# Forgetting attention of a decoder step: prompt and sample attention merged into one loop of 32 steps

## The reference, cut to what matters

```python
# prompt: 512 queries, causal
logits = einsum('bqhd,bkhd->bhqk', qb, k) * FOX_SCALE + cb[..., :, None] - cum[:, :, None, :]
logits = where(q_pos >= k_pos, logits, NEG_INF)
o = einsum('bhqk,bkhd->bqhd', softmax(logits), v)
# samples: 8 sequences x 4 queries against 2048 past keys (16 pages) and 4 new ones
k_past, v_past, lf_past = k_pool[page_table], v_pool[page_table], lf_pool[page_table]
suffix = reverse_cumsum(lf_all) - lf_all
logits = einsum('bqhd,bkhd->bhqk', q, k_all) * FOX_SCALE + suffix[:, :, None, :] - suffix[:, :, p_len:, None]
o = einsum('bhqk,bkhd->bqhd', softmax(where(mask, logits, NEG_INF)), v_all)
```

## Time and profile before

| | us |
|---|---|
| median of three runs | 3816.27 |
| the profiled execution | 3816.24 |
| its span, first to last instruction | 3814.6 |
| attention, first TensorE instruction at L1116 to the output projection's first at L668 | 1061.16 to 1684.47 |

### The profile page before, as it was taken

The page is one execution under the profiler, slowest core; times in us unless marked ns, Lnnn a source line. Parts: engine busy times, 40 slices in busy tenths (PEclk is TensorE's granted clock), DMA queues, the critical chain, the costliest instruction groups (busy, mean ns, idle before and its releaser), DMA issues.

```text
span 3814.6 us, 64314 instructions
## 1 busy us (share of the span) xinstructions
PE 3390.1 (89%) x26621; PEld 3033.2 (80%) x26621; DVE 1572.4 (41%) x2273; ACT 1059.2 (28%) x1437; POOL 240.9 (6%) x279
## 2 busy tenths in 40 slices
PE   7998899998999999988999866279999799889997
PEld 6897799988944466667999754179999698779997
DVE  2324544333134411226442379854432432464423
ACT  3301322222022244433222234342222320232222
POOL 0000000004300000000000057200000000000000
PEclk9996899999966699998999988689999899789998
DMA  3113232313110199962223211023232110422331
GB/s 93 56 34 111 72 88 87 92 53 84 38 48 1 56 377 393 392 246 68 86 87 91 55 44 44 12 67 88 87 91 76 56 51 27 124 70 85 88 91 46
DMA packets 465044, 367.67 MB, mean 96 GB/s; under 512 B 16329, under 2 KB 429438, under 8 KB 464924
## 3 DMA queue, kind: packets, MB, share of 16 engines
q1 hardware_dynamic: 449808, 348.72, 28.4%
q10 hardware_dynamic: 11020, 16.22, 1.2%
q0 software_dynamic: 4096, 1.06, 0.3%
HBM read 348.68 MB, written 17.26 MB: 96 GB/s over the span
## 4 chain that ended last, share of the span: by engine, by line
PE 82%; DVE 9%; issue 4%; ACT 3%; DVEq 0%; POOL 0%; DMA 0%; ACTq 0%; SPq 0%; POOLq 0%
PE acc L668 54%; PE acc L649 6%; PE acc L1005 3%; DVE big L1244 3%; PE acc L952 2%; PE acc L940 2%; PE acc L942 2%; PE acc L975 2%; PE acc L1044 2%; PE acc L864 2%; PE acc L852 1%; DVE rstd L1274 1%; PE acc L728 1%; ACT mix L2176 1%; PE acc L962 1%
## 5 line engine op out<-in xcount | busy, mean ns | idle before, releaser
L668 PE MATMUL acc<-h_hi,wsp 128*128 128x272 f32 x5632 | 943.3, 289 | 65.9 <-DVE h_lo L1530 65.9
L1266 DVE TENSOR_TENSOR wsp<-ring,wsp 128x1024 fp32r<-128x1024 f32 (+1 forms) x320 | 416.9, 1306 | 1164.2 <-ACT wsp L1893 1164.2
L668 PEld LDWEIGHTS acc<-h_hi,wsp 128*128 128x128 f32 x5632 | 797.9, 190 | 68.7 <-issue 68.4
L1893 ACT ACTIVATE wsp<-ring 128x1024 fp32r<-128x1024 f32 (+1 forms) x320 | 358.4, 1124 | 1297.6 <-PE acc L668 1294.5
L668 PE MATMUL acc<-h_lo,wsp 128*128 128x272 f32 x3328 | 690.0, 289 | 0.0
L668 PEld LDWEIGHTS acc<-h_lo,wsp 128*128 128x128 f32 x3328 | 527.3, 190 | 0.0
L668 PE MATMUL acc<-g_hi,wsp 128*128 128x272 f32 x2816 | 473.5, 290 | 24.0 <-DVE g_lo L1525 24.0
L668 PEld LDWEIGHTS acc<-g_hi,wsp 128*128 128x128 f32 x2816 | 400.9, 190 | 24.9 <-issue 24.9
L668 PE MATMUL acc<-i_hi,wsp 128*128 128x272 f32 x1536 | 265.1, 295 | 37.2 <-DVE i_lo L1294 32.4
L668 PE MATMUL acc<-g_lo,wsp 128*128 128x272 f32 x1408 | 292.4, 289 | 0.0
L668 PEld LDWEIGHTS acc<-i_hi,wsp 128*128 128x128 f32 x1536 | 224.8, 195 | 39.6 <-issue 35.5
(11 more groups left out here) (287 smaller groups left out, 3442.0 us busy)
## 6 DMA issues: line engine op xcount, KB each, us to landing
ring<-in_ffn_w SPq DMA_DIRECT2D x176, 512.0 KB, 3.8
mix<-in_cache_fox_k SPq DMA_DIRECT2D x96, 512.0 KB, 9.5
mix<-in_cache_fox_v SPq DMA_DIRECT2D x96, 512.0 KB, 10.2
ring<-in_ffn_w SPq DMA_DIRECT2D x64, 704.0 KB, 4.5
big<-in_cache_fox_k SPq DMA_DIRECT2D x32, 512.0 KB, 8.5
big<-in_cache_fox_v SPq DMA_DIRECT2D x32, 512.0 KB, 13.1
ring<-in_conv_w SPq DMA_DIRECT2D x24, 512.0 KB, 3.9
ring<-in_gla_wr SPq DMA_DIRECT2D x16, 512.0 KB, 3.7
```

Source lines behind the costliest of these rows:

```text
L668: last = pe.matmul(acc[:, bank + h, 0:HALF], wsp[:, s, w, k * P:(k + 1) * P], rhs[:, k0 + k, h * HALF:(h + 1) * HALF], start=start and k = ...
L1266: dve.tensor_tensor(wsp[:, s, 1, 0:tiles * P], ring[:, slot, 0:tiles * P], wsp[:, s, 0, 0:tiles * P], ALU.subtract).then_inc(wlo_done, 1)
L1893: act.activation(wsp[:, slot % SPLITS, 0, 0:tiles * P], ring[:, slot, 0:tiles * P], ACT.Copy)\
```

## The change

The two stages become one loop of 32 steps and 4 more. A step takes one pair of prompt items (two heads, one query block; the query blocks are now the outer loop, so the first 8 steps have 128 keys, the next 8 256, then 384 and 512) and four key pages of one sequence, and weighs the four value pages of four steps earlier. Of a key page, VectorE transposes 32 x 32 blocks (`turn_pages`), so that a head's 64 features lie in two blocks, and the scores of four pages come from 128 products of 32 rows and 32 columns of the array, 16 places in all (`sample_scores`). The forget sums come from a table `bias_all`, made once ahead of the loop and added by four products of 32 rows. The queries are repeated over the four partition groups and laid out in zeroed blocks by GpSimd (`query_blocks`), once for each sequence. The pages share a ring of 7 places, of which 5 are the weights' `ring`; the load of the output projection's weights now waits until all value pages are used. The mask of the prompt is added by a product with the identity instead of on VectorE; the scaling by the reciprocal moves to the copy of the result. Loops over sequences are written out.

```diff
 # SyncE
+for s in range(STEPS + LAG):
+    for g in range(GR):
+        if s < STEPS:
+            k_at[s * GR + g] = len(sequence)
+            sequence.append(("k", s * GR + g))
+        if s >= LAG:
+            v_at[(s - LAG) * GR + g] = len(sequence)
+            sequence.append(("v", (s - LAG) * GR + g))
 ...
+        for n, (kind, page) in enumerate(sequence):
+            if page % GR == 0:
+                sp.load(regs[kind], pt_sb[0:1, page:page + GR])
+                numbers[kind] = [sp.snap(r, min_val=0, max_val=NPOOL - 1) for r in regs[kind]]
+            if n >= RAW:
+                last_kind, last_page = sequence[n - RAW]
+                sp.wait_ge(turned if last_kind == "k" else v_used, last_page + 1)
+            cache = cache_k if kind == "k" else cache_v
+            sp.dma_start(raw(n), cache[0, ds(numbers[kind][page % GR], 1)].rearrange("a p h d -> p (a h d)"))\
+              .then_inc(raw_in[n % RAW], 16)
+        sp.wait_ge(v_used, DB * NPAGES)
                 load_out(w_view(fox_wo[0]))
 # TensorE
+    def scores_of_pair(s):
+        n = item(2 * s)[2]
+        q = n // P - 1
+        if s:
+            pe.wait_ge(pv_out, 2 * s)
 ...
+        for x in range(2):
+            h = item(2 * s + x)[1]
+            rows = slice(DH * x, DH * (x + 1))
+            pe.matmul(acc[:, 6 + x, 0:n], big[rows, h // 2, q * P:(q + 1) * P], big[rows, KD + h // 2, 0:n],
+                      start=True, stop=False, skip_group_check=True)
+        for x in range(2):
+            h = item(2 * s + x)[1]
+            pe.matmul(acc[:, 6 + x, 0:n], ident[0:FH, h:h + 1].to_broadcast([FH, P]), ncum[:, 0:n],
+                      start=False, stop=False, skip_group_check=True)
+            pe.matmul(acc[:, 6 + x, q * P:n], ident[:], causal[:], start=False, stop=True,
+                      skip_group_check=True).then_inc(sc_full, 1)
 ...
+    def sample_scores(s):
+        b, G = s // NG, s % NG
+        half = slice(32 * (b // 2), 32 * (b // 2 + 1))
+        pe.wait_ge(ksc_out, s)
+        pe.wait_ge(turned, GR * (s + 1))
+        if G == 0:
+            pe.wait_ge(qz_done, b + 2)
+        for a in range(GR):
+            at = a * NPAGES * 32 + G * P
+            pe.matmul(acc[:, a, 0:P], pick[half, b % 2].rearrange("p h i -> p (h i)"), bias_all[half, at:at + P],
+                      start=True, stop=False, skip_group_check=True, tile_position=(32 * (b // 2), 0))
 ...
+        for c in range(GH4):
+            for f in range(2):
+                cell = 2 * c + f
+                for a in range(GR):
+                    quad = slice(32 * a, 32 * (a + 1))
+                    for j in range(GR):
+                        h = GH4 * j + c
+                        at = (2 * h + f) * 32
+                        last = pe.matmul(acc[32 * j:32 * (j + 1), a, 0:P], qz[quad, b % 2, h, f, :],
+                                         kT[quad, :, at:at + 32], start=False, stop=(cell == 2 * GH4 - 1),
+                                         skip_group_check=True, tile_position=(32 * a, 32 * j))
 ...
+        last.then_inc(ksc_full, 1)
 ...
+    def weigh(v):
+        b, u = v // NG, v % NG
 ...
+        pe.wait_ge(pt_out, v + 1)
+        for g in range(GR):
+            page = v * GR + g
+            pe.wait_ge(*landed(v_at[page]))
+            for j in range(GR):
+                at = g * P + 32 * j
+                last = pe.matmul(acc[32 * j:32 * (j + 1), 5, 0:256], ptb[:, v % 2, at:at + 32],
+                                 raw(v_at[page])[:, j * 256:(j + 1) * 256], start=False,
+                                 stop=(u == NG - 1 and g == GR - 1), skip_group_check=True,
+                                 tile_position=(0, 32 * j))
+            last.then_inc(v_used, 1)
 ...
+    def attention():
+        for s in range(STEPS + LAG):
+            v = s - LAG
+            if s < STEPS:
+                if s % KD == 0 and s:
+                    rows_to_tiles(s)
+                scores_of_pair(s)
+            elif s == STEPS:
+                rows_to_tiles(s)
+            if v >= 0:
+                turn(v)
+            if v > 0 and v % NG == 0:
+                output(v // NG - 1)
+            if v >= 0:
+                weigh(v)
+            if s < STEPS:
+                sample_scores(s)
+                turn_pair(s)
+            if s < STEPS:
+                values_of_pair(s)
+        output(DB - 1)
 # VectorE
+    def turn_pages(s):
+        dve.wait_ge(ksc_full, s)
+        for g in range(GR):
+            n = k_at[s * GR + g]
+            dve.wait_ge(*landed(n))
+            dve.transpose(kT[:, g, :], raw(n)).then_inc(turned, 1)
+    def attention():
+        for s in range(STEPS + LAG):
+            v = s - LAG
+            if s < STEPS:
+                b, G = s // NG, s % NG
+                for x in range(2):
+                    n = item(2 * s + x)[2]
+                    dve.wait_ge(sc_full, 2 * s + x + 1)
+                    dve.tensor_reduce(nmax[:, x:x + 1], acc[:, 6 + x, 0:n], AX.X, ALU.max, negate=True)\
+                       .then_inc(pmax_done, 1)
+                dve.wait_ge(ksc_out, s + 1)
+                z = zs[b % 2]
 ...
+                step(dve.tensor_reduce(mx[:, b % 2, G:G + 1], z[:, G * GR * PAGE:(G + 1) * GR * PAGE], AX.X, ALU.max))
 ...
+                for x in range(2):
+                    dve.wait_ge(pexp_done, 2 * s + x + 1)
+                    dve.reciprocal(rsum[:, x:x + 1], rsum[:, x:x + 1]).then_inc(rinv_done, 1)
+                if s + 1 < STEPS:
+                    turn_pages(s + 1)
 ...
 # ScalarE
+        for s in range(STEPS + LAG):
+            v = s - LAG
+            if s < STEPS:
+                for x in range(2):
+                    n = item(2 * s + x)[2]
+                    act.wait_ge(pmax_done, 2 * s + x + 1)
+                    act.activation(probs[x][:, 0:n], acc[:, 6 + x, 0:n], ACT.Exp, bias=nmax[:, x:x + 1],
+                                   accum_out=rsum[:, x:x + 1]).then_inc(pexp_done, 1)
+            if v >= 0:
 ...
+                act.wait_ge(pt_full, v + 1)
+                if v >= 2:
+                    act.wait_ge(v_used, GR * (v - 1))
+                act.activation(ptb[:, v % 2, :], acc[:, 4, :], ACT.Copy).then_inc(pt_out, 1)
+            if s < STEPS:
+                b, G = s // NG, s % NG
+                z = zs[b % 2]
+                act.wait_ge(ksc_full, s + 1)
 ...
+                act.activation(z[:, G * GR * PAGE:(G + 1) * GR * PAGE].rearrange("p (g a s) -> p a g s", g=GR, a=GR),
+                               acc[:, 0:GR, 0:P].rearrange("p a (g s) -> p a g s", g=GR), ACT.Copy)\
+                   .then_inc(ksc_out, 1)
 ...
+                for x in range(2):
+                    n = item(2 * s + x)[2]
+                    act.wait_ge(tr_full, 2 * s + x + 1)
+                    act.activation(pT[:, x, 0:n], acc[:, 6 + x, 0:n], ACT.Copy).then_inc(tr_out, 1)
+                if G == NG - 1:
+                    act.wait_ge(nmx_done, b + 1)
+                    act.wait_ge(ksc_out, s + 1)
+                    act.activation(z, z, ACT.Exp, bias=nmx[:, b % 2:b % 2 + 1],
+                                   accum_out=ssum[:, b % 2:b % 2 + 1]).then_inc(zexp_done, 1)
+                for x in range(2):
+                    q, h, n = item(2 * s + x)
+                    act.wait_ge(pv_full, 2 * s + x + 1)
+                    act.wait_ge(rinv_done, 2 * s + x + 1)
+                    act.activation(o_nat[:, h * DH:(h + 1) * DH], acc[:, 6 + x, 0:DH], ACT.Copy,
+                                   scale=rsum[:, x:x + 1]).then_inc(pv_out, 1)
 ...
```

More of the change, by code:

```diff
@@ L292, in build @@
         lf_in = sem("lf_in")
-        pages_in = [[sem(f"pages_in{half}_{s}") for s in range(8)] for half in range(2)]
+        raw_in = [sem(f"raw_in{r}") for r in range(RAW)]
         nat_out = sem("nat_out")
@@ L1782, in fox @@
+                dve.tensor_tensor(bias_all[:, KEYS:ZN].rearrange("p (b i) -> p b i", b=DB), own_b[:],
+                                  sums[:, NPAGES:NPAGES + DS].rearrange("p (b i) -> p b i", b=1).to_broadcast([P, DB, DS]),
+                                  ALU.add).then_inc(bias_done, 1)
+                turn_pages(0)
+                attention()
                 low(0, KD, t.split + 1)
```

711 lines of the change are left out of this document (268 added, 443 removed).

## The result

The changed kernel takes 4055.45 us (median, 4053.22 to 4061.86) against 3816.01 of the kernel before on the same chip: 1.0629 times as long, 95% interval 1.0611 to 1.0647. That is +239 us where +34 was forecast, beyond the range (3755 to 3985). Of the profiled execution (span 4055.4), attention runs from 1061.82, the first product at L1143, to 1925.03, the output projection's first L695: 863.2 us against 623.3.

What follows compares the result with a forecast made beforehand. Two attention stages with opposite limits were to merge into a loop paced by each step's semaphore chain. Terms summed to 656.7 us of attention against 623.3, +33.4 on 3816.24: 3850 us, range 3755 to 3985.

Steps and rivals of the forecast that it cites:

- then the 128 small products: Key scores in each step: 256 records at 16.25 ns each, 4.2 us; called the largest unknown.
- the sum: Chain of an ordinary step: 17.2, 17.5, 18.6 and 20.4 us for 128, 256, 384 and 512 keys.
- The path of a step: VectorE's transposes and ScalarE's exponentials set the step; TensorE's prompt pair late at 512 keys, 0.7 us added at 384.
- little work: Old prompt stage: 64 items follow one another through four engines, so 257 us pass with little work.
- the eight page transfers (10.8) hide under each: Loop: a step's eight page transfers, 10.8 us, stay covered unless steps fall below that.
- The third rival: Loop at clock 0.62 because TensorE idles 6 to 8 us a step: +116 us, 3966; chance 0.15.
- Four pages: Weighing four value pages in a step: 2.9 us, between 1.93 in mid-loop and 3.64 after idle; third rival 3.6.
- The bias: Four bias products a step: 1.4 us, range 1.0 to 2.9; third rival 2.9.
- weighing ahead of the scores gains nothing: Loop: value pages wait for a copy behind the exponentials, so weighing starts after the block transposes, not beside them.
- setup, first steps, block transposes: Ahead of the loop 22.8 us, first step 10.6, three steps without weighing 41; a block transpose 1.15.
- First and second rivals: Small products: all 16 places side by side, 3774 us, chance 0.30; only four strips overlap, 3952, chance 0.17.
- Changes of sequence: Loop: 2.5 us at each of seven changes, with 1.6 for new keys in eight steps: 30 us.

Runs made afterwards that it cites:

- e1_loop: Changed kernel with a step's small products as a loop of 7 turns plus 16 products, all on the first cell's operands (scores incomplete): 3891.48 us.
- e8: e1_loop with 3 turns instead of 7, so 64 small products a step instead of 128: 3880.1 us.
- e5: Changed kernel with a step's key scores ahead of its value pages on TensorE again: 4009.31 us.
- e13: e5 with a step's four key pages asked for ahead of its four value pages instead of in turn, same seven places: 3873.26 us.
- e16: Changed kernel, values still weighed ahead of scores, with only the page order of e13 (keys asked for first): 4020.01 us.
- e15_keys_first_loop: e13 with the prompt pair's transposes ahead of the value pages and the small-product loop of e1_loop (scores incomplete): 3792.69 us.
- e4: Changed kernel with the value pages' copy ahead of the exponentials on ScalarE and their transposes ahead of the prompt pair on TensorE: 4034.46 us.
- e3: Changed kernel with a page asked for only when the third before it has landed, at most three under way instead of seven: 4028.83 us.

## Why the prediction was wrong

The sign was right; the size was not, and the chain set the pace at most in the steps of 128 keys. Four steps of the prediction failed.

**The step "then the 128 small products".** I asked what the engine takes in per record and took 4.2 us. In the row of the stop 165 records pass in 2.36 us, 14 ns each, at a granted clock of 0.87, and elsewhere 256 in 5.4 at half clock, 21 ns each; over all steps L1029 is busy 158.2 us, 4.9 a step. The term was 4.2 against 4.9, well placed. (The Trainium skill, "TensorE: Matmul & The Clock Gate", Part 1, "Wait — 56ns, not 53.3ns?", has some 25 ns as the least; this trace goes below it.) What I did not price is that the code for them must arrive: the change writes 36 steps out in line, and the sum had no term for it. It cost 104 us of stops, and e1_loop, with a quarter of that code, took away 165 us of the loop.

**The path of a step.** The sum lets VectorE's transposes and ScalarE's exponentials set the step, adds 0.7 us for TensorE's prompt pair at 384 keys, and puts the pair on the path at 512 keys alone, at 1.6 us for its values and 4.7 for scores and masks. In the trace TensorE sets the step from 256 keys on. VectorE's maxima wait for the product that adds the mask (L972), the last of an item's scores, in 48 of 64 cases:

```profile
DVE big L1627 <- PE acc L972: 101.9, 48, 5.3
```

And TensorE goes from the pair's values (L990) to the transposes of the next weighing (L1056) with one wait of 0.40 us, here with 256 keys and with 512:

```profile
1354.57 1.97 PE L990 MATMUL acc<-mix 128*128 128x64 f32 x8
1356.94 1.23 PE L966 MATMUL acc<-big 64*128 64x256 f32 x4 [0.40 <-ACT big L2146]
...
1361.70 1.06 PE L1056 MATMUL acc<-ident,yT 128*128 128x128 f32 x4
...
1806.04 3.67 PE L990 MATMUL acc<-mix 128*128 128x64 f32 x16
1810.12 2.08 PE L966 MATMUL acc<-big 64*128 64x512 f32 x4 [0.40 <-ACT big L2146]
...
1817.44 1.06 PE L1056 MATMUL acc<-ident,yT 128*128 128x128 f32 x4
```

With 512 keys the values take 3.7 us and scores and masks 7.3, together 11.0 where the sum has 6.3. So steps exceed the sum by 3.7, 5.8, 7.7 and 8.0 us for 128 to 512 keys, while the stops are some 3.5 of each. The row of the prompt stage had a sign of it: TensorE busy 248.89 of 257 us at clock 0.62, which I read as "little work".

**The step "the eight page transfers (10.8) hide under each".** They fit by their sum but not by their places. I compared 10.8 us with 17 and didn't ask when a place comes free. Seven places for eight pages, asked for in turn, make the transfers one burst between weighing and scores. In e8 and e5 that burst is on the path; in the changed kernel it lay on the instruction supply instead. e13 shows its worth: 136 us by order of pages alone, once the scores stand ahead (35 in the changed kernel's order, e16).

**The third rival, "the loop runs at the prompt stage's clock",** had 0.15, and its clock came true: 0.58 in the 28 steps against 0.62 there. Four pages took 3.6 us against 2.9, as the rival priced them, and the pair at 512 keys took longer by more than its 3 us. The bias took 1.6 to 2.0 against 1.4, not its 2.9; L864, from which I had 1.9, ran at half clock itself (0.50 from 285.0 to 288.7). Its +116 and the stops' 104 together give some 4070, near the measured 4055; but e1_loop, still at 0.68, came within 33 us of the forecast's loop (625 against 592), so how much is the clock's is not settled. Its reason, idle time of TensorE, is not what the rows show: in e15_keys_first_loop TensorE is busy 460 of 487 us at a clock of 0.73.

**Right:** that weighing ahead of the scores gains nothing (undone: -46, with keys first -147, though 82 and 55 us fewer stops are in these); setup, first steps, block transposes. The reason was only partly so: the exponentials ahead of `pt_out` were worth 20 us (e4), not the 2 to 3 us a step that I put on them; from 256 keys on TensorE itself is late, which the sum had for 512 keys and in part for 384.

**First and second rivals:** the 16 places do work beside each other to a degree (29 ns a product at a high clock, where four strips alone would give 57.5); neither end was reached. Changes of sequence were under-priced: they make steps 4 to 8 us longer, 39 us in all against 30.

## What to carry to other kernels

When a loop is written out in line, count its instructions for each engine and the traffic they have to pass: here a stop without a releaser, in the midst of a run of short instructions while DMA is full, was the engine waiting for its code, and the times of the instruction queue's packets showed it. Look at each engine's busy time before you call a stage one of little work. When pages share places, write down for each page whose place it takes and when that one is done; a sum of transfer times says nothing until this is known. Two orders that depend on each other have to be changed together: each of these two alone was worth a fifth to a quarter of what both were.

## What the runs showed of the hardware

The granted clock fell to half in the midst of small products without any idle time: in e1_loop TensorE is busy throughout the two stretches below, inside one run of L1029 (first line), and PEclk goes from 1.00 to 0.50 (2.4 to 1.2 GHz).

```profile
1514.41 4.83 PE L1029 MATMUL acc<-mix 32*32 32x128 f32 x256
...
1515.00:1516.00 1.00, 1.00 (x73) 0.53 (x77) 0.00 (x0) 0.00 (x0) 0.00 (x0) 1.00 1.00 184
1517.00:1518.00 1.00, 1.00 (x73) 0.82 (x64) 0.00 (x0) 0.00 (x0) 0.00 (x0) 0.50 0.97 397
```

I had expected the clock to fall by idle time only. And asking for fewer pages at once (e3: three) made each land sooner (4.7 to 5.0 us against 5.8 to 6.9), while the stops lost only 17 of 104 us.
